# Seven products for 18 of 22 halves of a down projection, and stores of two products at a time

## What is computed

```python
D_FF = 5632
h = rmsnorm(x, pre_ffn_g[l])
up = causal_depthwise_conv(h @ w_up[l], conv_w[l], conv_b[l])
gate, val = jnp.split(up, 2, axis=-1)
y = (jax.nn.gelu(gate, approximate=True) * val) @ w_down[l]
x = x + rmsnorm(y, post_ffn_g[l])
```

## Time and profile before

| | us |
|---|---|
| median of 3 runs | 2611.43 (2610.83 to 2612.22) |
| profiled execution | 2610.45 |
| its span, first to last instruction | 2608.70 |
| PE busy | 2596.3 |
| DVE busy | 1891.1 |
| ACT busy | 1145.7 |
| POOL busy | 198.6 |

### The profile page before, as it was taken

How to read it: one execution, slowest core, us unless ns; L and a number is a source line. 1 busy time by engine, 2 the same in 40 slices (tenths; PEclk the granted TensorE clock), 3 DMA queues, 4 the chain that set the end, 5 groups by cost and what they waited for, 6 DMA issues and landing times.

```text
span 2608.7 us, 44288 instructions
## 1 busy us (share of the span) xinstructions
PE 2596.3 (100%) x18036; PEld 2431.5 (93%) x18036; DVE 1891.1 (72%) x2673; ACT 1145.7 (44%) x1540; POOL 198.6 (8%) x273
## 2 busy tenths in 40 slices
PE   9999999999999999999999999999999999999998
PEld 8999999999999888888999999999999999999997
DVE  8897888787878545336796667677777767677777
ACT  8443434443444322234454444444444444444443
POOL 0100000000000100000001111111111111111111
PEclk9999999999999999999999999999999999999999
DMA  6434343334343833434246555555555555555567
GB/s 250 142 117 142 115 135 124 110 118 126 104 152 125 319 129 129 152 129 154 82 125 137 140 136 134 138 138 130 138 134 133 137 130 137 137 132 143 131 148 272
DMA packets 107659, 372.03 MB, mean 143 GB/s; under 512 B 12448, under 2 KB 12448, under 8 KB 101584
## 3 DMA queue, kind: packets, MB, share of 16 engines
q1 hardware_dynamic: 72864, 264.28, 31.6%
q0 software_dynamic: 34608, 105.06, 18.1%
HBM read 297.98 MB, written 67.11 MB: 140 GB/s over the span
## 4 chain that ended last, share of the span: by engine, by line
PE 93%; DVE 4%; DMA 1%; issue 1%; ACT 0%; SPq 0%; DVEq 0%; ACTq 0%
PE ps L643 30%; PE ps L644 30%; PE ps L645 30%; PE ps L735 1%; DMA mixing<-in_x 1%; PE ps L682 1%; PE ps L725 1%; DMA w_raw<-in_w 1%; DVE big L2105 0%; DVE w_hl L2046 0%; PE ps L709 0%; DVE w_hl L2040 0%; DVE rm_lo L1589 0%; DVE w_hl L1643 0%; DVE w_hl L1636 0%
## 5 line engine op out<-in xcount | busy, mean ns | idle before, releaser
L643 PE MATMUL ps<-h_hi,w_hl 128*128 128x256 f32 (+1 forms) x2032 | 611.8, 301 | 0.7 <-DVE mixing L1664 0.3
L645 PE MATMUL ps<-h_hi,w_hl 128*128 128x256 f32 (+1 forms) x2032 | 605.5, 298 | 0.0
L644 PE MATMUL ps<-h_lo,w_hl 128*128 128x256 f32 (+1 forms) x2032 | 605.4, 298 | 0.0
L643 PE MATMUL ps<-w_hl,h_hi 128*128 128x512 f32 (+1 forms) x1168 | 433.3, 371 | 1.8 <-DVE h_lo L1572 1.3
L644 PE MATMUL ps<-w_hl,h_hi 128*128 128x512 f32 (+1 forms) x1168 | 429.1, 367 | 0.0
L645 PE MATMUL ps<-w_hl,h_lo 128*128 128x512 f32 (+1 forms) x1168 | 428.9, 367 | 0.0
L643 PEld LDWEIGHTS ps<-h_hi,w_hl 128*128 128x128 f32 x2032 | 388.6, 191 | 16.5 <-DVE w_hl L1643 1.7
L644 PEld LDWEIGHTS ps<-h_lo,w_hl 128*128 128x128 f32 x2032 | 388.6, 191 | 13.4 <-issue 1.0
L645 PEld LDWEIGHTS ps<-h_hi,w_hl 128*128 128x128 f32 x2032 | 388.5, 191 | 11.1
L1093 ACT ACTIVATE w_hl<-w_raw 128x768 fp32r<-128x768 f32 x152 | 128.6, 846 | 444.8 <-PE ps L645 444.6
L1349 ACT ACTIVATE w_hl<-w_raw 128x768 fp32r<-128x768 f32 x168 | 142.1, 846 | 407.8 <-PE ps L645 407.8
(11 more groups left out here) (272 smaller groups left out, 5637.3 us busy)
## 6 DMA issues: line engine op xcount, KB each, us to landing
w_raw<-in_w SPq DMA_DIRECT2D x487, 512.0 KB, 3.5
y_scratch<-work POOLq DMA_DIRECT2D x160, 256.0 KB, 5.8
gate_scratch<-mixing POOLq DMA_DIRECT2D x8, 1024.0 KB, 6.6
mixing<-in_x POOLq DMA_DIRECT2D x4, 1024.0 KB, 6.8
mixing<-mixing POOLq DMA_DIRECT2D x16, 256.0 KB, 3.5
merged<-gate_scratch POOLq DMA_DIRECT2D x4, 1024.0 KB, 13.8
g_ret<-gate_scratch POOLq DMA_DIRECT2D x4, 1024.0 KB, 13.8
y_scratch<-work POOLq DMA_DIRECT2D x8, 512.0 KB, 20.4
```

The lines of the kernel that those rows point to most:

```text
L643: pe.matmul(bank, s_hi, m_hi_, start=first, stop=False, skip_group_check=skip)
L644: pe.matmul(bank, s_hi, m_lo_, start=False, stop=False, skip_group_check=skip)
L645: return pe.matmul(bank, s_lo, m_hi_, start=False, stop=last, skip_group_check=skip)
```

## The change

The down projection of groups 0 to 8 (18 halves of the loop) is computed with seven products too. A half is now two blocks (`sub`) of 512 output columns, each of two chunks; every chunk takes a round of sums, two high and two low parts, as in the up projection, so a half has 12 like rounds (`quad_half`). The sums' signs differ. The activations are split as blocks and forms (`first_forms`, `make_forms`, `second_form`, `third_forms`), six splits for four. The seven products of a block go each to a PSUM bank, 14 copies per half instead of 8 (`leave_product`), and are added up over the groups as products in `y7_scratch`, seven times 512 columns a row. The order in which they are copied lets pairs of neighbours go by one store of 512 KB in rows of 4 KB; each seventh goes alone (`STORES`). The first group's stores write, the others accumulate; the clears go. Beside the last quad half and the two plain halves POOL combines the products in DRAM, by loads and accumulating stores (`fetch_*`, `move_*`). Group 9's down projection stays plain and adds its tiles in pieces of 1 KB; the last group's is unchanged. Staging slots are 14, two of them the space of `gbuf`, two that of `vbufs[0]`, five that of the forms; `gate_linear` and others wait for their stores. DRAM loads of y at the end come in 16 pieces. The descriptor scratch shrinks to 2048 bytes, and the room goes to the forms.

```diff
+QUAD_HALVES = HALVES - 2
+QUAD_GROUPS = QUAD_HALVES // 2
+SUB = 2
+STAGE = ((2, 3, 4, 5, 0, 1, 6, 7, 8, 3, 2, 4, 5, 6), (2, 3, 0, 1, 4, 5, 6, 2, 3, 10, 9, 11, 12, 13))
+ADDED = (0, 0, 1, 1, 2, 2, 3, 4, 4, 5, 5, 5, 5, 5)
+PLAIN_ADDED = {2: 1, 3: 6, 4: 2, 5: 7, 6: 3}
+STORES = ((0, 2), (2, 2), (4, 2), (6, 1))
...
+SUB_BANKS = ((7, P1, Q6, P2, Q7, Q4, Q3), (Q5, 7, P1, Q6, P2, Q7, Q4))
+LEAVE = ((0, 1, 2, 3, 4, 5, 6), (0, 2, 3, 4, 5, 6, 1))
+DOWN_ORDER = ((P1, Q6, P2, Q3, Q4, Q7, Q5), (P1, Q5, Q6, Q7, Q4, P2, Q3))
+AFTER_SUBS = (Q3, Q5, P1, Q6, P2, Q7, Q4)
+C11, C12, C21, C22 = P2, Q3, Q4, Q7
+PLACE = {P1: 0, Q6: 1, C11: 2, C12: 3, C21: 4, C22: 5, Q5: 6}
+MOVED_0, MOVED_1, MOVED_2 = 4, 12, 16
...
-        staged = [part(1024 + t * NB, NB) for t in range(TT)]
+        staged = [gbuf[:, 0, :], gbuf[:, 1, :]] + [part(1024 + t * NB, NB) for t in range(TT)] +                  [at("staged_6", -2, [NB])[:, :]] + [part(t * NB, NB) for t in range(2)]
+        f1_hi, f1_lo = at("f1_hi", -14, [2, S], F32R), at("f1_lo", -10, [2, S], F32R)
+        s4_hi, s4_lo = at("s4_hi", -6, [2, HB], F32R), at("s4_lo", -4, [2, HB], F32R)
+        forms_f32 = at("forms_f32", -14, [6, NB])
...
+            def accumulate_products(g, e):
+                for sub in range(SUB):
+                    for j, count in STORES:
+                        n = left_before(half_index(g, e)) + 7 * sub + j
+                        pool.wait_ge(y_left, n + count)
+                        products = [DOWN_ORDER[sub][k] for k in LEAVE[sub][j:j + count]]
+                        slot = min(stage(n + i) for i in range(count))
+                        src = staged_pair(slot) if count == 2 else staged[slot]
+                        target = y_range(SUB * e + sub, min(products, key=PLACE.get), count)
+                        landed = y_added[counter_of(n)]
+                        if g == 1:
+                            pool.dma_start(target, src).then_inc(landed, 16)
+                        else:
+                            pool.dma_start(target, src, accum_op=ALU.add).then_inc(landed, 16)
...
+            for g in range(1, QUAD_GROUPS + 1):
+                for e in range(2):
+                    if (g, e) == (QUAD_GROUPS, 1):
+                        added(left_before(QUAD_HALVES - 1))
+                        fetch_first(0)
+                        pool.wait_ge(product_back, back_seen + 16 * 4)
+                        move_first(0)
+                    accumulate_products(g, e)
...
+            added(left_before(QUAD_HALVES))
+            pool.wait_ge(product_moved, moved_seen + 16 * MOVED_0)
+            fetch_first(1)
+            fetch_second(0)
+            pool.wait_ge(product_back, back_seen + 16 * 12)
+            move_first(1)
+            move_second(0)
+            pool.wait_ge(product_moved, moved_seen + 16 * MOVED_1)
+            move_third(0)
+            pool.wait_ge(product_moved, moved_seen + 16 * MOVED_2)
+            for dd in range(2):
+                accumulate_plain(0, dd)
+            fetch_second(1)
+            pool.wait_ge(product_back, back_seen + 16 * 16)
+            move_second(1)
+            pool.wait_ge(product_moved, moved_seen + 16 * (MOVED_2 + 4))
+            move_third(1)
+            pool.wait_ge(product_moved, moved_seen + 16 * (MOVED_2 + 8))
             pool.wait_ge(chunk_used, C_LAST - 2 * DOWN)
-            early, late = slice(0, D // 2), slice(D // 2, D)
+            added(left_before(HALVES - 1))
             for t in range(2):
...
+                if t == 0:
+                    added(ALL_LEFT)
+                load_y(t, 2 if t < 2 else 0, ND)
...
+            def down_quads(c, s, w, act_count):
+                pe.wait_ge(act_lo, act_count)
+                e, left = s * 7 - 7, left_before(w)
+                waits = (((y_left, left), (p1_left, s), (u_step, e + 1), (u_step, e + 2), (u_step, e + 3),
+                          (u_step, e + 4), (u_step, e + 5)),
+                         ((u_step, e + 7),) + tuple((y_left, left + k) for k in range(1, 7)))
+                for sub in range(SUB):
+                    for i in range(SUB):
+                        pe.wait_ge(lo_ready, c + SUB * sub + i + 1)
+                        w_h, w_l = quad_split(i)
+                        for k, p in enumerate(DOWN_ORDER[sub]):
+                            if i == 0 and (waits[sub][k][0] is not y_left or waits[sub][k][1]):
+                                pe.wait_ge(*waits[sub][k])
+                            bank, col = ps[SUB_BANKS[sub][k]], slice(COLUMN[p] * HB, COLUMN[p] * HB + HB)
+                            o_h, o_l = down_operand(p, i)
+                            for m in range(2):
+                                tok = slice(m * P, m * P + P)
+                                mm = passes(bank[:, m * HB:m * HB + HB], (o_h[:, tok], o_l[:, tok]),
+                                            (w_h[:, col], w_l[:, col]), i == 0 and m == 0, i == SUB - 1, True)
+                            if i == SUB - 1 and k < 6:
+                                mm.then_inc(y_done, 1)
+                        mm.then_inc(chunk_used, 1)
...
+                act.wait_ge(g_tap0, s * 2)
+                if s > 1:
+                    act.wait_ge(act_lo, splits_before(s // 2))
...
+                if g:
+                    act.wait_ge(y_added[0], 16 * stores(left_before(half_index(g, e) + 1), 0))
...
+            def leave(n, bank, scale=1.0):
+                counter = counter_of(n)
+                if counter not in (0, 4, 5) and stores(n, counter):
+                    act.wait_ge(y_added[counter], 16 * stores(n, counter))
+                if n == left_before(QUAD_HALVES - 1):
+                    act.wait_ge(product_moved, moved_seen + 16 * MOVED_0)
+                if n == left_before(QUAD_HALVES):
+                    act.wait_ge(product_moved, moved_seen + 16 * MOVED_1)
+                act.activation(staged[stage(n)], bank, ACT.Copy, scale=scale).then_inc(y_left, 1)
+            def leave_product(g, e, sub, j):
+                w, k = half_index(g, e), LEAVE[sub][j]
+                if k < 6:
+                    act.wait_ge(y_done, done_before(w) + 6 * sub + k + 1)
+                else:
+                    act.wait_ge(chunk_used, half_chunk_0(g, e) + KH + SUB * sub + SUB)
+                if sub == 0 and j == 0:
+                    act.wait_ge(prod_ready, 2 * (2 * g + e))
+                leave(left_before(w) + 7 * sub + j, ps[SUB_BANKS[sub][k]][:, :], -1.0 if DOWN_ORDER[sub][k] in (Q4, Q5) else 1.0)
...
+            def quad_half(g, e, tasks):
+
+                c, n, s = half_chunk_0(g, e), sums_before(g, e), 2 * g + e
+                leaves = {KH: lambda: leave_p1(s),
+                          KH + 2: lambda: [leave_product(g, e, 0, j) for j in range(5)],
+                          KH + 3: lambda: [leave_product(g, e, 0, j) for j in (5, 6)],
+                          KH + 4: lambda: [leave_product(g, e, 1, j) for j in range(3)],
+                          KH + 5: lambda: [leave_product(g, e, 1, j) for j in range(3, 7)]}
+                for i in range(2, PER_HALF + 2):
+                    quad_hi(c, i, c + (i - 1))
+                    quad_sum_hi(n + i, i)
+                    if i in leaves:
+                        leaves[i]()
+                    if i in tasks:
+                        tasks[i]()
+                    if e and i == KH + 4:
+                        gate_linear(g, e)
+
+            quad_half(1, 0, {2: lambda: gate_linear(0, 1), 3: lambda: val_linear(0, 1), 4: lambda: gelus(1),
+                             5: lambda: first_forms_hi(0, C_SUB1), 7: lambda: [second_form_hi(0), third_forms_hi(0)]})
+            for g in range(1, QUAD_GROUPS + 1):
+                if g > 1:
+                    quad_half(g, 0, {2: lambda: val_linear(g - 1, 1), 3: lambda: gelus(2 * g - 1),
+                                     4: lambda: first_forms_hi(g - 1, half_chunk_0(g, 0)),
+                                     6: lambda: second_form_hi(g - 1), 7: lambda: third_forms_hi(g - 1)})
+                quad_half(g, 1, {2: lambda: gate_linear(g, 0), 3: lambda: val_linear(g, 0), 4: lambda: gelus(2 * g)})
 
             def after_sub(g, e, c, h, following, after_gates=None):
...
+                b12 = raw[:, 0:HB].unsqueeze(1).to_broadcast([P, 2, HB])
+                TTm(v[:, 0, :].rearrange("p (a s) -> p a s", a=2), raw[:, HB:3 * HB].rearrange("p (a s) -> p a s", a=2),
+                    b12, ALU.subtract if for_down(i) else ALU.add).then_inc(sum_ready, 1)
...
+            def first_forms_lo(g):
+                for j, (a, src, c) in enumerate(((0, 0, slice(0, HB)), (2, 1, slice(0, HB)), (4, 1, slice(HB, S)))):
+                    dve.wait_ge(act_hi, splits_before(g) + j + 1)
+                    hi, lo = late_pieces(a)
+                    TTm(lo, vbufs[src][:, :, c], hi.bitcast(F32), ALU.subtract).then_inc(act_lo, 1)
...
+            def make_forms(g, steps):
```

(36 more changed lines are left out.)

310 lines of the change are left out of this document (202 added, 108 removed).

## The result

The changed kernel takes 2629.07 us (median, 2625.94 to 2631.08), the kernel before took 2611.82 beside it: a ratio of 1.0067, 95% interval 1.0055 to 1.0079. I had forecast 2603 with a range of 2587 to 2615. The profiled execution took 2631.08 us; its span is 20.7 us longer than that of before.

A forecast was written before the change was run, and what follows sets the result against it. TensorE (PE), busy for 2596.3 of 2608.7 us, was taken as the bound. -29.2 + 7.6 - 0.5 + 2.4 + 2.2 + 7.2 + 1.5 = -8.8 us gave 2601.6 profiled, about 2603 as median, range 2587 to 2615.

The forecast's parts named there:

- PE's stream: Down projections: 168 matmuls of 256 columns replace 96 of 512, 1.62 us less per half, 29.2 us over 18 halves.
- Tap pairs: Two tap tasks in adjacent rounds make DVE late for PE: 19 x 0.40 us = 7.6 us.
- First half and recombination: Recombining in even halves costs 2.4 us, loop half one's squeezed rounds 2.2 us; two old holes go, -0.5 us.
- gate_linear: In odd halves ACT waits there for a 512 KB store, delaying PE beyond 9.3 us: 9 x 0.8 = 7.2 us.
- Slot reuse: In the loop, leaves wait for the store that empties their slot; named as a new wait, given no cost.
- The chain in the tail: Loads and adds combining products, about 35 us long beside 40 us of up projection: hidden, no cost.
- the last weight loads: In the tail, slower adds beside these loads delay PE by 0 to 7.6 us; 1.5 us taken.
- Descriptor scratch: Shrinks from the default to 2048 bytes; costed at nothing, with at most eight stores in a half.
- The port rule for descriptors: GpSimd cannot write DMA descriptors while VectorE holds the shared port: 11 us more; left out of the sum.
- The slower rival: Odd halves' second store lands late, with 5 us more in the tail or the port rule: 2617 to 2625; chance 0.13.
- D: Landing time of an odd half's second store; PE loses (D - 9.3) x 1.25 in nine halves, deciding from 10.7 us.

The follow-up runs named there:

- e_best: e_pool with the edits of e_slot and e_spread, and gate_linear behind two of the four leaves of round KH + 5; 2594.7 us.
- e_slot: Changed kernel, but in even halves the single product of the first block is copied and stored first; 2623.3 us.
- e_spread: Changed kernel, but in odd halves value taps and products move to rounds 4 and 6, ACT's linear and gelu parts to 4 and 5; 2625.9 us.
- e_gate: Changed kernel, but gate_linear of odd halves stands one round later, ahead of that round's leaves; 2626.2 us.
- e_nomoves: Changed kernel without the tail's chain of loads and adding stores and the waits for it, so the output lacks these terms; 2613.5 us.
- e_ring4: Changed kernel with slot 6 done without (its store sends a constant tile) and descriptor scratch 4096 bytes in place of 2048; 2624.7 us.
- e_pool: Changed kernel, but POOL combines the tail's products on chip: 16 products loaded and 16 added, one round trip for each quarter; 2615.6 us.
- e_noadd: e_best without POOL's three adds and one copy per quarter, so the blocks get plain products; 2590.8 us.
- e_single: Changed kernel, but each paired 512 KB store leaves as two stores of 256 KB in rows of 2 KB; 2641.5 us.

## Why the prediction was wrong

- **PE's stream (-29.2): right.** 18 x 1.62 us, by the 120 ns pitch; e_best shows 20.16 us in 17 of 18 downs. (The count of 96 matmuls of before is 2 x 4 x 4 x 3; the "4 x 4 x 4 x 3" of the prediction is a slip, which the sum doesn't use.) By an estimate from the gaps of the Trainium skill (TensorE: Matmul & The Clock Gate, Back-to-back issue gap) it would be 18.35; no run shows that.
- **Tap pairs (0.40 each): right in size.** e_slot, where nothing else is late, shows 0.44 behind an even half. e_spread with it shows that the pair can be undone at no cost.
- **First half and recombination (2.4 + 2.2, less 0.5): about right.** 1.8 in eight even downs (0.23 each, at chunk 10 as counted), and 1.6 + 1.1 around the first down where my terms leave 2.1.
- **gate_linear (7.2): the mechanism right, the size 5.8.** Of the 9.7 us behind odd halves 9 x 0.43 are the taps' and 5.8 this wait's. The wait occurs in eight halves and not in nine, since the first group's stores only write: there the store lands 6.7 us after its issue. In the eight it lands 9.1 to 10.3 us after (9.6 in the mean), and PE pays what goes beyond about 8.9 us, one for one, where I had 9.3. e_gate shows that the instruction's place counts too: one round later there is no wait, and its own 1.5 us cost as much.
- **Slot reuse (nothing): the failed step in the loop.** I wrote that leaves wait for the store that empties their slot, and priced only gate_linear's. Slot 6, listed in the same way, has 9.95 us from the store's issue to its need, and that store is the fourth in a row and landed after 12.9. It costs 12.2 us behind even halves (16.2 in the changed kernel, 4.0 in e_slot). With it, the forecast's 18.9 us of losses in the loop become 31.1; the trace has 30.5 (16.2 + 9.7 + 3.0 + 1.6).
- **The chain in the tail ("hidden"): the failed step of the sum, 19.7 against 1.5.** Two things were wrong. Its deadline: I set it against the 40 us of up projection, but the plain half's first copy waits for two thirds of the batch's adding stores and its first store for all of them. ACT came to that copy at 2478.16 (2492.90 less its wait), 27 us after the batch's first load at 2451.55. Its length: 51 us to 2502.24 against my 35, since I took landings of single stores, while here twelve products meet at the engines at once (97% busy, 1.57 us each). e_nomoves shows that it is the chain, e_ring4 that it isn't the scratch, and e_pool that a shorter chain frees it; that the length is the engines' time is read from their 97%, not from a run of its own. The 1.5 us that I did price in the tail, for the last weight loads, are not there: what follows the third stretch takes 45.9 us, before it took 46.8.
- **Descriptor scratch (nothing): right within 2.3 us, for another reason.** POOL was held 17.63 us, which I had not counted on; but e_ring4 shows that with 4096 bytes the same time is spent waiting for landings. The default size was not tried.
- **The port rule for descriptors, 11 us: not seen.** DVE is busy for 79% now, and the issue of an adding store in the loop takes 0.84 to 1.21 us, in the median 0.85 (1.05 for those from slot 6). The rule is that of the Trainium skill (SBUF — State Buffer, SBUF: two separate sides), and it speaks of DVE in a 2-port mode; no run shows DVE in such a mode here, so it is not refuted.
- **The slower rival** had the right sign and kind (a store lands after a slot is needed) and the wrong store: its condition D > 10.7 us at gate_linear was not met (9.6 in the mean), slot 6 and the chain were not in it, and 2629 lies above its 2617 to 2625 too.

## What to carry over

When products are parked in few slots, list for every reuse the time from the store's issue to the need, not only for the one that looks new, and count a store's landing from its place in its queue. A chain of loads and adding stores has the deadline of the first instruction queued behind it, and with many products in flight single landings are no measure of its length; fewer products and round trips gained 13.5 us where moving them gained nothing. A better shape of the transfers shows in the time only while a wait for them reaches the engine that bounds the kernel.

## What the runs showed of the hardware

- POOL's elementwise additions and DVE's two-input operations slow each other: DVE from 0.41 to 1.51 us and from 1.22 to 2.31 us, POOL from 1.29 to 4.43 us, this last once (e_pool). The Trainium skill (SBUF — State Buffer, Who interferes with whom) says that a DVE instruction with two SBUF inputs contends with a GpSimd instruction that reads SBUF; the trace agrees. It cost 3.9 us here (e_noadd).
- After PE had worked 0.13 of 5.50 us, its granted clock in the next 5.20 us was 0.50, the 1.2 GHz level: 24 matmuls took 5.20 us where 24 x 0.12 = 2.9 is usual. So a hole of 5.5 us costs about 2.3 us more than itself. In the stretch from 2501.80 on, the holes behind the first (0.95, 0.52, 1.21 and 1.38 us, with 0.1 us for the restart behind each) and the clock make up the 6.8 us.
- Adding costs the DMA engines twice what writing does. Per 256 KB they needed 0.71 us in the changed kernel's first group, whose stores write (16.5% of the 120 us from 1360 to 1480, for 28 products), and 1.42 us from 1480 on, where they add. The 512 KB stores of slots 0 and 1 landed after 5.9 and 6.7 us in the first group and after 9.1 to 11.8 us later.
- An adding store of 256 KB took the 16 engines 1.91 us in the kernel before, 1.42 us per 256 KB in the changed one and 1.53 us in e_single, whose stores have the same size and rows as those of before; what makes the difference to before (the row's place in DRAM, the 14 KB distance of rows) was not tried.
